# Layer one's output product: eight row blocks as four seven-product pairs, with sums written in place

## The reference

```python
ym = _mem_attention(qm.reshape(B, T, M_HEADS, M_HDIM), mk, mv).reshape(B, T, M_WIDTH) * jax.nn.silu(zm)
out = jnp.concatenate([y_mix, ym], axis=-1) @ w_out
x = x + _rmsnorm(out, p['g_post'][l])
```

## Time and profile before

| | us |
|---|---|
| median of 3 runs | 1755.72 (1755.45 to 1756.52) |
| the profiled execution, device time | 1758.04 |
| its span in the profile | 1756.3 |
| PE busy in the span | 1741.5 |
| DVE, ACT, POOL busy | 872.8, 595.0, 499.3 |
| first of layer one's output products | starts at 732.35 |
| first of layer two's products | starts at 913.53 |
| first product of layer two's second pair of units | starts at 938.83 |

### The profile page before, as it was taken

The page is one execution under the profiler, slowest core; times in us unless marked ns, Lnnn a source line. Parts: engine busy times, 40 slices in busy tenths (PEclk is TensorE's granted clock), DMA queues, the critical chain, the costliest instruction groups (busy, mean ns, idle before and its releaser), DMA issues.

```text
span 1756.3 us, 22816 instructions
## 1 busy us (share of the span) xinstructions
PE 1741.5 (99%) x8470; PEld 1353.8 (77%) x8470; DVE 872.8 (50%) x1801; ACT 595.0 (34%) x1445; POOL 499.3 (28%) x539
## 2 busy tenths in 40 slices
PE   9999999999999999999999999999999999999998
PEld 5577766888788888747558888888888888889643
DVE  0444423776666556451333443355335544565775
ACT  1421234564565234311221233432333234533312
POOL 0151100335232012410003543145414643122640
PEclk9999999999999999999999999999999999999999
DMA  8311111246755235541111111323123343745333
GB/s 271 138 61 66 66 45 50 55 151 158 230 171 166 85 100 164 178 147 48 50 58 57 41 48 45 99 88 96 50 73 117 97 148 109 266 146 181 132 108 110
DMA packets 149081, 196.25 MB, mean 112 GB/s; under 512 B 19083, under 2 KB 108171, under 8 KB 148834
## 3 DMA queue, kind: packets, MB, share of 16 engines
q1 hardware_dynamic: 140708, 174.58, 31.3%
q10 hardware_dynamic: 8262, 20.20, 3.3%
HBM read 156.97 MB, written 37.85 MB: 111 GB/s over the span
## 4 chain that ended last, share of the span: by engine, by line
PE 90%; DVE 3%; issue 3%; ACT 1%; DMA 1%; POOL 1%; SPq 0%; DVEq 0%; ACTq 0%; POOLq 0%
PE PS L3547 50%; PE PS L2289 7%; PE PS L2439 6%; PE PS L2079 3%; PE PS L575 3%; PE PS L401 3%; PE PS L2530 2%; PE PS L2115 2%; PE PS L2090 2%; PE PS L296 2%; PE PS L2112 2%; PE PS L925 1%; DVE WK L732 1%; PE PS L918 1%; PE PS L3445 1%
## 5 line engine op out<-in xcount | busy, mean ns | idle before, releaser
L3547 PE MATMUL PS<-HT,RING 128*128 128x258 f32 (+2 forms) x1776 | 445.6, 382 | 0.3 <-ACT WK L3637 0.3
L3547 PEld LDWEIGHTS PS<-HT,RING 128*128 128x128 f32 x1776 | 328.5, 190 | 48.0 <-issue 4.1
L3637 ACT ACTIVATE BIG<-PS 128x256 f32<-128x256 f32 (+2 forms) x140 | 53.7, 384 | 375.2 <-PE PS L3547 375.1
L3547 PE MATMUL PS<-BIG,RING 128*128 128x258 f32 (+1 forms) x656 | 159.7, 382 | 0.9 <-DVE BIG L3731 0.9
L3547 PEld LDWEIGHTS PS<-BIG,RING 128*128 128x128 f32 x656 | 123.0, 190 | 19.1 <-DVE BIG L3731 1.3
L3547 PE MATMUL PS<-BIG,WK 128*128 128x258 f32 (+1 forms) x448 | 113.7, 383 | 0.0
L3547 PE MATMUL PS<-HT,CST 128*128 128x256 f32 (+2 forms) x432 | 110.2, 382 | 0.1
L3547 PEld LDWEIGHTS PS<-BIG,WK 128*128 128x128 f32 x448 | 82.7, 190 | 14.0 <-issue 3.0
L3547 PEld LDWEIGHTS PS<-HT,CST 128*128 128x128 f32 x432 | 79.6, 190 | 11.4 <-DVE BIG L3736 0.9
L575 PE MATMUL PS<-WK,RING 128*128 128x344 f32 x288 | 84.3, 453 | 0.1
L3733 DVE TENSOR_TENSOR BIG<-BIG,PS 128x256 f32<-128x256 f32 (+1 forms) x70 | 29.5, 422 | 103.6 <-PE PS L3547 103.4
(11 more groups left out here) (455 smaller groups left out, 3270.6 us busy)
## 6 DMA issues: line engine op xcount, KB each, us to landing
RING<-in_w_in_a SPq DMA_DIRECT2D x14, 1024.0 KB, 6.7
WK<-in_cache_mem_kv SPq DMA_DIRECT2D x56, 256.0 KB, 5.6
RING<-in_w_kv_b SPq DMA_DIRECT2D x12, 1024.0 KB, 5.2
RING<-in_w_in_b SPq DMA_DIRECT2D x12, 1024.0 KB, 5.3
WK<-in_cache_win SPq DMA_DIRECT2D x40, 256.0 KB, 5.4
RING<-in_w_mkv SPq DMA_DIRECT2D x16, 512.0 KB, 4.9
BIG<-in_x_prompt SPq DMA_DIRECT2D x16, 512.0 KB
BIG<-sample_query SPq DMA_DIRECT2D x28, 256.0 KB, 5.8
```

The costliest lines, as they stand in the source:

```text
L3547: last = nc.tensor.matmul(PS[:, bank, 0:mid - lo], weight_block(u // 2, s, k), h_block(layer_of(u), u % 2, t, k), start=(k == 0 and j not ...
L3637: nc.scalar.activation(part(u, n2 if j == 0 else n1, lo, mid), PS[:, banks(u)[0], 0:mid - lo], ACT.Copy).then_inc(sig("projections_copied" ...
```

## The change

Layer one's output takes layer two's row order and its scheme: blocks (0, 1), (2, 3), then the sample block, (4, 5) and (6, 7) as four pairs. A pair's feature tiles are split 6 + 6, so each of seven products is six matmuls of 512 columns. Four row sums a pair are made on DVE, each as two instructions (two tiles and four tiles), S1, S2 and S4 in place of the rows that they replace. Four weight sums of six tiles are made on POOL, T1, T2 and part of T4 in place. The first product of each pair is copied by ACT out of PSUM. The sample rows are multiplied in four 32-column groups into one bank. Two block turns are now woven into layer two's first products, with the norms and copies that belong to them.

```diff
+            if s == S3:
+                dve.wait_ge(sig("ym_ready").sem, 4)
...
+            for n in range(2):
+                last = nc.vector.tensor_tensor(out[n], x[n], y[n], op)
+            last.then_inc(sig("sums_by_dve").up(), 1)
...
+            if t == T3:
+                pool.wait_ge(*product_done(UA - 1, NPROD - 1))
+                pool.wait_ge(sig("out_weights_loaded").sem, 80)
+                pool.wait_ge(sig("late_weights_loaded").sem, 128)
+            elif t == T1:
+                pool.wait_ge(sig("sample_rows_done").sem, 1)
...
+            x, y = {T3: (B22, T1), T1: (T1, B11), T2: (B22, T1), T4: (T2, B21)}[t]
+            for k in (0, 1, 5, 2, 3, 4):
+                if t == T4 and k == 2:
+                    pool.wait_ge(*pair_product_done("A", OUT_PAIRS[0], 4))
+                last = nc.gpsimd.tensor_tensor(weight_tile(t, k), weight_tile(x, k), weight_tile(y, k), ALU.subtract)
+            last.then_inc(sig("pair_weights_summed").up(), 1)
...
+            pe.wait_ge(sig("late_weights_loaded").sem, 128)
+            for p in OUT_PAIRS:
+                pair_product(pe, x, p, 0, range(5, 6))
+            pe.wait_ge(sig("small_read").sem, SMP[x]["small"]["sp"])
+            sample_rows_pe(pe, x, range(8))
+            pe.wait_ge(sig("ym_ready").sem, 4)
+            for n, p in enumerate(OUT_PAIRS):
+                pair_product(pe, x, p, 2)
+                value(2 * n)
+                value(2 * n + 1)
+            pair_product(pe, x, p0, 4)
+            sample_out_pe(pe, x)
+            pair_product(pe, x, p0, 1)
+            sample_rows_pe(pe, x, range(8, 12))
+            pair_product(pe, x, p0, 3)
...
+            block_turn(pe, x, 1)
+            pair_product(pe, x, p1, 6)
+            pair_product(pe, x, p2, 1)
+            pair_product(pe, x, p2, 4)
+            block_turn(pe, x, 2)
+            pair_product(pe, x, p2, 3)
+            block_turn(pe, x, 3)
...
+            block_turn(pe, x, 6)
+            pair_product(pe, x, p3, 6)
...
+            for n in range(6):
+                value(n)
+            rows(p0, S3)
+            rows(p0, S1)
+            value(6)
+            value(7)
+            rows(p0, S2)
+            rows(p0, S4)
...
+            block_dve(dve, x, 3)
+            pair(p2, U2)
+            block_norm_dve(dve, x, 3)
+            row_sums_dve_a(dve, p3)
+            block_all_dve(dve, x, 4)
             h_copy_dve(dve, x, 2)
...
+            h_sum(dve, "B", 0, T1)
+            h_sum(dve, "B", 0, T2)
+            block_dve(dve, x, 7)
+            pair(p3, C12)
+            h_sum(dve, "B", 0, T3)
+            h_sum(dve, "B", 0, T4)
             block_dve(dve, x, 8)
...
+            for t in (T3, T1, T2):
+                weight_sum_pool_a(pool, t)
             scale_pair(pool, PA)
             sum_pair(pool, PA)
+            weight_sum_pool_a(pool, T4)
             scale_pair(pool, PA + 1)
...
-            if x == 4:
-                block_turn(pe, "A", 8)
+            if x in (3, 6):
+                block_turn(pe, "A", (7, 8)[x == 6])
```

More of the change, by code:

```diff
@@ L2439, in pair_product @@
-                last = nc.tensor.matmul(PS[:, bank, :], x, w, start=(k == 0 and j not in (2, 3, 6)), stop=(k == 3),
+                if x == "A":
+                    y, w = row_tile(i, s, k), weight_tile(t, k)
+                else:
+                    y = row_sum(i, s)[:, k] if s in (S1, S2, S3, S4) else c.src(k if s == A11 else 4 + k, rows.start, rows.stop)
+                    if t in (T1, T2, T3, T4):
+                        w = weight_sum(t)[:, k]
+                    else:
+                        w = c.piece(k if t == B11 else 4 + k)
+                        w = w[:, 512:D] if t == B22 else w[:, 0:512]
@@ L2440, in pair_product, with pair_copied @@
+                last = nc.tensor.matmul(PS[:, bank, :], y, w, start=(k == 0 and j not in (2, 3, 6)), stop=(k == nk - 1),
                                         skip_group_check=True)
-            if ks[-1] == 3:
+            if ks[-1] == nk - 1:
                 last.then_inc(sig("projections_done").up(), 1)
[L2444 to L2452, removed]
+        def pair_copied(x, i):
+            n = 2 * UA if x == "A" else 2 * NUNIT + len(OUT_PAIRS)
+            return sig("projections_copied").sem, n + OUT_PAIRS.index(i) + 1
@@ L2502, in sample_rows_pe, with sample_rows_bank @@
+        def sample_rows_bank(x):
+            return 6 if x == "A" else 7
+        def sample_rows_pe(pe, x, kts):
+            c = OUT[x]
+            if kts[-1] == c.kts - 1:
+                pe.wait_ge(sig("sample_out_read").sem, SMP[x]["order"] + 1)
+            for kt in kts:
                 for q in range(4):
-                    last = nc.tensor.matmul(PS[32 * q:32 * q + NS, 7, 0:256], c.src(kt, T, W),
+                    last = nc.tensor.matmul(PS[32 * q:32 * q + NS, sample_rows_bank(x), 0:256], c.src(kt, T, W),
@@ L2578, in out_pe @@
-            ym = 0
-            pe.wait_ge(sig("ym_ready").sem, ym + 1)
-            pe.wait_ge(*weights1)
-            for i in range(2):
-                block_products(pe, x, i, late, value(i))
-            pe.wait_ge(sig("ym_ready").sem, ym + 4)
-            hold = turns({6: (0,), 11: (1,)})
-            last = value(2)
-            def both(kt):
-                last(kt)
-                if kt == TURN_SAMPLES[x]:
-                    sample_out_pe(pe, x)
-                hold(kt)
-            block_products(pe, x, 2, late, both)
```

540 lines of the change are left out of this document (296 added, 244 removed), and 4 rows, old and new, of the table PAIR_ORDER_A.

## The result

In five runs of each kernel the changed one took 1763.29 us in the median (1762.29 to 1764.59) and the kernel before 1755.84: a ratio of 1.0039, 95% interval 1.0029 to 1.0050. The change makes the kernel slower, by 7.5 us. The forecast was slower by 4.0, at 1759.7: the direction held, and the size was 3.5 us short. The measured median lies near the upper end of the stated range (1764.5) and just above what the prediction called the forecast's own (1757 to 1763).

The account below looks back on a forecast made before the run. The prediction took PE's work to bound the kernel, with nobody keeping PE waiting. Its terms, −19.5 + 12.6 + 0.9 + 3.8 + 6.2, gave +4.0 us, a median of 1759.7, with a range of 1750.5 to 1764.5.

Parts of the forecast that it names:

- the forecast's own: Whole kernel: the case that the forecast's terms hold, with waits of 21 to 26 us, at 1757 to 1763 us; chance 0.43.
- PE's work: PE in layer one's output: rows and column turns taken out, less pair products and sample matmuls added, give −19.5 us.
- The wait for the values: PE at the sample values: DVE takes turns with POOL at 1.69 an instruction, so values come late, +12.6 us.
- U2: First pair on DVE: U2 stands behind the second pair's row sums, beside POOL's T4, and PE wants the banks: +0.9 us.
- The turn of block 3: PE waits there for DVE's copy of block 2's turn, which now stands behind two blocks: +3.8 us (0 to 6).
- The last two blocks: Layer two's start: +3.9 us at turn 7, then waits at the second unit for turn 8's copy and HT sums; +6.2 in all.
- The clock: PE over the whole span: read at full clock before the change, and given no term in the sum.
- same: Whole kernel: a median between 1752.2 and 1759.2 us, as a measurement can tell about 0.2%; chance 0.34.
- Looser turns: Rival at DVE's values beside POOL: 1.56 an instruction, sum +0.6 us, 1756.3, no change; chance 0.33.
- Cheap POOL: Rival at the values: POOL costs DVE little, eighth value before 781, total −9.5 us, 1746.2; decided by 789; chance 0.16.
- A lock for whole instructions: Rival at the values: DVE and POOL exclude each other, 1.95 for each of the first 18, +4.7 us, 1764.4; chance 0.08.

Follow-up runs that it names:

- e7: e6 plus PE taking values 4 to 7 later and DVE copying block 3's turn and making U2 earlier: 1743.13 us, ratio 0.9917 to the kernel before.
- e8: e7 with DVE's copy of block 8's turn and a first HT sum ahead of the first unit's last output sum: 1741.66 us, ratio 0.9905 to before.
- e3: Changed kernel with POOL's weight sum T4 ahead of scaling and summing layer two's first weights: ratio 0.9998 to the kernel before.
- e4: Changed kernel with each of POOL's four weight sums making one tile instead of six, the other work left out: one run, 1748.82 us.
- e2: Changed kernel with the copies of block 2's turn moved earlier on DVE and ACT: 1759.34 us, ratio 1.0015 to the kernel before.
- e5: Changed kernel with block 7's norm ahead of block 8, and block 8's squares and scaling behind layer two's first copy and sum: 1760.65 us, ratio 1.0017.
- e1: Changed kernel with extra matmuls of unused result put in PE's waits for values and before block 3's turn: 1760.28 us, ratio 1.0018 to the kernel before.
- e0: Changed kernel without any edit, run again on the same chip as the next three: ratio 1.0039 to the kernel before.
- e6: Changed kernel with the edits of e2, e3 and e5 together: 1749.57 us, ratio 0.9954 to the kernel before.

## Why the prediction was right, and where it was short

In the first profile the stretch grew by 6.7 us where +4.0 was forecast. The mechanism was right: PE saves some 19 us of work and waits for more than that, at the places that were named. The size was short by a term that the sum put at nothing, PE's clock. By the prediction's own steps:

- **PE's work, −19.5.** The counts are the 336 and 96 rows that were forecast. Its size shows best where waits are few and the clock is full: the rest is 188.1 and 187.9 (e7, e8) against 206.5, so −18.5. Short by about 1. These two runs still hold seven or eight new waits, and eight rows behind a wait take 1.99 in place of 1.89; whether that makes up the 1 us was not tried apart. PE busy was to fall by 19 to 20 us and fell by 13.6, since the rows at the lower clock count as busy.
- **The wait for the values, +12.6: measured 9.8.** The mechanism is shown three ways: by 3.43 + 1.64 in the trace, by e3 (13.2 to 5.8 us with POOL still) and by e4 (no wait). The price per instruction, 1.69, was right from the third value on. What was missed is that the first two values would be cheap: the sixth was ready 27.4 us after DVE's start, not 30.4. The second value is 2.0 of this, by POOL's pause before T1. The last weights had landed 12.4 us after their issue, not 13.9; by the forecast's landing and prices T3 would have lasted to 758.2, past PE's sample rows, and without a pause (an estimate). The first value is 0.8, which the prediction had seen at 1660.24 and not counted in. The ten behind took 13.2, not 12.4. PE's own time up to the values came out nearly right by two small errors: the wait of 0.5 lies ahead of 732.35 and was counted again, and two short products (L1855 and L1871, some 0.5 together) were left out.
- **U2, +0.9: 0.7.** **The turn of block 3, +3.8: 4.0,** from the copy that was named (e2).
- **The last two blocks, +6.2: 5.9.** The two at the second unit are those forecast, 1.2 and 1.5 for 1.2 and 1.1. The 3.9 at turn 7 came as two others, 3.2 together: 1.4 for ACT's first copy of layer two, behind block 8's squares, and 1.8 for DVE's first sum of layer two, behind block 8's chain and block 7's norm. Turn 7 itself did not wait. The cause is the chain that was named, but what PE met first was not (e5).
- **The clock, 0: measured +4.9.** This is the step that failed. The prediction read full clock over the whole span of before and carried its paces over, though it forecast 23.5 us of waiting for the same PE. e1 shows that the clock falls because PE stands still there.

The sum in place of +4.0: −18.5 + 9.8 + 0.7 + 4.0 + 5.9 + 4.9 = +6.8, near the 6.7 of the stretch and the 0.39% of the medians.

Some of the agreement is luck. Without the clock the same sum is +1.9, and e1_fill, where the clock stays full, lies at +1.7 in the stretch and 0.18% in the median, inside what the prediction called "same". So that the change came out clearly slower is owed to the one term that was not in the sum; the value wait, 2.8 too high, covered more than half of what was missing.

The rivals. Looser turns (1.56 an instruction) fell as a price: from the third value on the rows say 1.68. As a size they were nearer than the forecast: the six values took 27.4 us, 1.52 an instruction on average, and the wait of 9.8 lies closer to this rival's 9.2 (12.6 less 3.4) than to 12.6. Cheap POOL fell: the eighth value was ready at 790.6. Its other half, that the kernel gains once that value is ready by 789, is not shown by e3, where it was ready at 781.4 and the kernel was level (0.9998), with 5.6 us of lower clock; e4, with the values ready at 776.9, had a stretch 7.3 below that of before, in one run that leaves work out. A lock for whole instructions would have made 1.95 of each: the values beside POOL's sums have 1.68, so the rule of the Trainium skill, page "SBUF — State Buffer", section "Who interferes with whom", holds here in its first half (the two contend) and is too strict in its second (an exclusive lock).

What stays open: why the clock fell after a wait of 2.88 us in e0 and of 1.39 in e6, and not after one of 3.05 in the first profile and of 1.40 in e2, was not tried apart.

## What to carry to other kernels

A cut in the bound engine's work is worth its size only if the helpers' work that pays for it fits beside it: here 18.5 us saved on PE brought 20.4 us of waits, nearly all for DVE, and 4.9 us of lower clock, and order alone (what stands ahead of what on DVE, ACT, POOL and PE) turned +0.4% into −0.95%. When a forecast holds waits of several microseconds on PE, add what the work behind them costs at the lower clock (3.2 and 1.7 us at the two places of the first profile); and place added two-input work on POOL where DVE has nothing of that kind that PE waits for.

## What the runs showed that was not expected

- PE at 0.50 for about 10 us around waits of 4.0 and 2.7 us, and for some 3 us after another of 4.0: 4.9 us of loss on top of 20.4 us of waits. 28 rows of useless matmuls in the waits gave 5.0 us back.
- One wait of 2.9 us was enough for it (e3): the ten rows behind it took 2.9 us longer, so that removing two waits of three gave back 6.2 us where 9.9 was counted on.
- The reordering on PE, 2.1 us alone, came with two small ones to 6.9 us once the other waits were gone, since then the clock held over the whole stretch.
